# Twelve V buffers in three groups, two more query-weight slices streamed per tile, and a fourth V group in the last two U segments

## The reference, cut to what matters

```python
q = einsum('bsd,de->bse', h, w_query)                 # 1024 -> 2048
scores = einsum('bshpd,hpnd->bshpn', q, sub_keys)     # 8 heads x 2 x 128 keys
...                                                   # top 16 of each, top 16 of their sums
expert = i1 * N_KEYS + i2                             # 8 x 16 = 128 experts for a token
gates = softmax(best)
u = take(expert_u, expert)                            # 128 rows of 1024 floats for a token
act = gelu(einsum('tkd,td->tk', u, x)) * gates
out = einsum('tk,tkd->td', act, take(expert_v, expert))   # another 128 rows of 1024 floats
```

## Time and profile before

| | |
|---|---|
| median of 3 runs | 3504.99 us (3499.11 to 3507.13) |
| the profiled execution | span 3777.3 us; no other time of this execution is given |
| busy, of the span | PE 2191.6 us (58%), DVE 2151.9 (57%), POOL 2096.8 (56%), ACT 384.3 (10%) |
| moved by DMA | 1195.92 MB, mean 317 GB/s |

### The profile page before, as it was taken

One profiled execution on the slowest core, in us unless ns is written; L12 is line 12 of the kernel. 1 busy time (PEld: TensorE's weight loads), 2 busy tenths in 40 slices (PEclk: granted clock), 3 DMA queues, 4 the chain that ended last, 5 costly groups with the idle time before them and its releaser, 6 DMA issues. The chain is left out here.

```text
span 3777.3 us, 34501 instructions
## 1 busy us (share of the span) xinstructions
PE 2191.6 (58%) x9905; PEld 1104.5 (29%) x9905; DVE 2151.9 (57%) x6670; ACT 384.3 (10%) x701; POOL 2096.8 (56%) x2079
## 2 busy tenths in 40 slices
PE   6899968747646656635665455556654333333345
PEld 4666655324233233212321232134211000100111
DVE  4333577565667777568656775667666644444300
ACT  2322132111010010001000100010000000000000
POOL 1000056545635566666666657666666766666664
PEclk9999989877767768766766677756776556555676
DMA  8423288877959899989999999999999999999997
GB/s 281 139 66 102 86 276 328 308 266 283 345 184 330 286 336 378 403 325 352 357 403 353 358 335 404 373 341 354 409 344 360 366 362 363 359 373 361 358 363 296
DMA packets 412550, 1195.92 MB, mean 317 GB/s; under 512 B 58993, under 2 KB 135106, under 8 KB 410434
## 3 DMA queue, kind: packets, MB, share of 16 engines
q0 software_dynamic: 294912, 1073.87, 75.6%
q1 hardware_dynamic: 39970, 75.66, 5.6%
q10 hardware_dynamic: 77472, 44.08, 4.1%
HBM read 1172.46 MB, written 21.00 MB: 316 GB/s over the span
## 5 line engine op out<-in xcount | busy, mean ns | idle before, releaser
L998 POOL DMA_INDIRECT U<-in_expert_u,eidx x1024 | 1054.8, 1030 | 575.6 <-issue 287.5
L1380 PE MATMUL bank<-V,ZH 128*32 128x512 f32 x3712 | 726.3, 897 | 915.9 <-DMA V<-in_expert_v,eidxT 727.5
L2159 DVE CUSTOM_DVE_ANT_0 U<-U,h1c 128x512 f32<-128x512 f32 x1368 | 871.8, 690 | 532.6 <-DMA U<-in_expert_u,eidx 393.7
L1006 POOL DMA_INDIRECT V<-in_expert_v,eidxT x832 | 842.7, 1013 | 499.9 <-POOLq L1004 249.2
L1380 PEld LDWEIGHTS bank<-V,ZH 128*32 128x32 f32 x3712 | 142.0, 142 | 1403.9 <-issue 1401.8
L2148 DVE CUSTOM_DVE_ANT_0 U<-U,h1c 128x1024 f32<-128x1024 f32 x256 | 303.2, 1224 | 67.5 <-DMA U<-in_expert_u,eidx 42.7
L310 PE MATMUL bank<-V,U 128*128 128x387 f32 (+2 forms) x928 | 278.4, 459 | 10.6 <-PEq L308 10.5
L1028 POOL COPY eidx<-eidx_n 128x128 uint32<-128x128 uint32 x8 | 3.3, 413 | 413.9 <-POOLq L1027 413.2
L1185 PE MATMUL bank<-wq,arena 128*128 128x512 f32 x400 | 194.1, 634 | 28.7 <-PEq L1308 18.4
L310 PEld LDWEIGHTS bank<-V,U 128*128 128x128 f32 x928 | 178.9, 196 | 100.5 <-issue 21.6
L372 DVE SCALAR_TENSOR_TENSOR U<-bank,U 128x384 f32<-128x384 f32 (+3 forms) x108 | 61.8, 572 | 127.8 <-DVEq L367 117.2
(11 more groups left out here) (308 smaller groups left out, 2834.6 us busy)
## 6 DMA issues: line engine op xcount, KB each, us to landing
arena<-in_w_out SPq DMA_DIRECT2D x56, 512.0 KB
U<-in_w_in ACTq DMA_DIRECT2D x36, 512.0 KB, 3.9
U<-in_expert_u,eidx POOLq DMA_INDIRECT x1024
V<-in_expert_v,eidxT POOLq DMA_INDIRECT x928
raw<-proj_dram SPq DMA_DIRECT2D x8, 1344.0 KB
wq<-in_w_query SPq DMA_DIRECT2D x4, 2048.0 KB, 15.5
proj_dram<-U ACTq DMA_DIRECT2D x35, 192.0 KB, 1.9
arena<-w_dram SPq DMA_DIRECT2D x6, 1024.0 KB
```

The costliest lines, as they stand in the source:

```text
L998: pool.indirect_dma_start(U[:, c % NU, :], None, expert_u[0], rows(ap=eidx[:, e, c:c + 1], axis=0)).then_inc(g_u[c % NU], 16)
L1006: pool.indirect_dma_start(V[:, c % NV, :], None, expert_v[0], rows(ap=eidxT[:, e, token:token + 1], axis=0)).then_inc(g_v[c % NV // 2], 16)
L1380: last = nc.tensor.matmul(acc_ps[NSTEP * j:NSTEP * j + NSTEP, 512 * n:512 * n + 512], Zb[:, at - i:at - i + NSTEP], buf[j][:, 512 * n:512 ...
L2159: ins = nc.vector.tensor_tensor_reduce(out=U[:, c % NU, lo:lo + D // 2], in0=U[:, c % NU, lo:lo + D // 2], in1=rows[:, lo:lo + D // 2], sc ...
```

## The change

Four things change together. (1) V has 12 buffers in three groups: `V` itself (groups 0 and 1) and the place of `wq`'s slices 5 and 6 (group 2). The table `MIXED_RING` gives the group of each of a tile's 32 steps: 0, 1, 2 by turns up to step 28, then 0, 1, 2, so that the steps 27 to 30 are groups 0, 1, 0, 1. (2) Slices 5, 6 and 7 are all kept in `w_dram` (3 MB, `LEAN` = 3), and each of tiles 2 to 7 reads three slices back instead of one: four transfers where there was one, ahead of the fifth `wo` load, and two more after the last `wo` load, behind a new wait for the second `wo` buffer. PE gives that buffer free after k = 5 too, and waits before `route` for all six. (3) In the last two U segments (V of tiles 5 and 6) the steps go round four groups; the fourth is the first 4096 floats of `arena`, whose token DVE gives when the loop of U segments 2 to 5 is over. (4) ACT's last `fill` of a tile waits for its own end before it tells PE, and SP waits for `s_x_free` too before it loads `wq`.

```diff
+MIXED_RING = [i % 3 for i in range(29)] + [0, 1, 2]
+LAST_RING = [i % 4 for i in range(NSTEP)]
+NRING = 4
+LEAN = 3
...
+def ring_of(t, i):
+
+    return LAST_RING[i] if isinstance(t, int) and t >= T - 3 else MIXED_RING[i]
+
...
-        w_dram = nc.dram_tensor("w_dram", (P, 2 * PH * P), fp32).ap()
+        w_dram = nc.dram_tensor("w_dram", (P, LEAN, 2 * PH * P), fp32).ap()
...
-        w_part = view(1024, 2 * PH * P)
+        w_last, w_next = view(1024, 2 * PH * P), [view(4608, 2 * 512), view(7168, 2 * 512)]
+        w_third = [view(3584, 2 * 512), view(6656, 512), view(3072, 512)]
+
+        def w_read(k, group):
+
+            if k == KD - 1:
+                return w_last[:, 512 * group:512 * group + 512]
+            if k == KD - 2:
+                return w_next[group // 2][:, 512 * (group % 2):512 * (group % 2) + 512]
+            if k == KD - 3:
+                return w_third[0][:, 512 * group:512 * group + 512] if group < 2 else w_third[group - 1]
         Lists = namedtuple("Lists", "top itop ftop cand cid best ibest fbest fex den eq first eq_first")
 
...
+        v_rows = [V[:, 0:4, :], V[:, 4:8, :], wq[:, KD - LEAN:KD - 1, :].rearrange("p k (b d) -> p (k b) d", d=D),
+                  view(0, 4, D)]
...
-                            sp.dma_start(w_part, w_dram[:, :]).then_inc(w_in, 16)
+                            sp.dma_start(w_last, w_dram[:, 2, :]).then_inc(w_in, 16)
+                            sp.dma_start(w_next[0], w_dram[:, 1, 0:1024]).then_inc(w_in, 16)
+                            sp.dma_start(w_next[1], w_dram[:, 1, 1024:2048]).then_inc(w_in, 16)
+                            sp.dma_start(w_third[2], w_dram[:, 0, 1536:2048]).then_inc(w_in, 16)
...
+                    sp.wait_ge(b_wo_free1, 1)
+                    sp.sem_inc(b_wo_free1, -1)
+                    if streamed(t):
+                        sp.dma_start(w_third[0], w_dram[:, 0, 0:1024]).then_inc(w_in, 16)
+                        sp.dma_start(w_third[1], w_dram[:, 0, 1024:1536]).then_inc(w_in, 16)
...
-                def v_row(e, c):
+                def v_row(e, c, ring):
+                    r = ring[c // 4]
                     if c % 4 == 0:
-                        pool.wait_ge(g_vfree[c // 4 % 2], 1)
-                        pool.sem_inc(g_vfree[c // 4 % 2], -1)
+                        pool.wait_ge(g_vfree[r], 1)
+                        pool.sem_inc(g_vfree[r], -1)
                     token = c % 4 * NSTEP + c // 4
-                    pool.indirect_dma_start(V[:, c % NV, :], None, expert_v[0],
-                                            rows(ap=eidxT[:, e, token:token + 1], axis=0)).then_inc(g_v[c % NV // 2], 16)
+                    pool.indirect_dma_start(v_rows[r][:, c % 4, :], None, expert_v[0],
+                                            rows(ap=eidxT[:, e, token:token + 1], axis=0)).then_inc(g_v[2 * r + c % 4 // 2], 16)
 
...
+                with pool.Fori(0, T // 2 - 2):
                     for e in range(2):
-                        next_slots(e)
-                        for q in range(P // 4):
-                            for c in range(4 * q, 4 * q + 4):
...
-                        if k < KD - 3:
+                        if k < KD - 2:
...
-                        pe.wait_ge(w_in, 16)
-                        pe.sem_inc(w_in, -16)
+                        pe.wait_ge(w_in, 16 * 6)
+                        pe.sem_inc(w_in, -16 * 6)
                     for k in range(4 * half, 4 * half + 4):
-                        w = w_part if from_dram and k == KD - 1 else wq[:, k, :]
-                        last = nc.tensor.matmul(o, h1T[:, k, :], w[:, 512 * group:512 * group + 512], start=k == 0, stop=k == KD - 1)
+                        w = w_read(k, group) if from_dram and k >= KD - LEAN else wq[:, k, 512 * group:512 * group + 512]
...
+                    r = i % 2 if wide else ring_of(t, i)
+                    buf = [(U[:, 4 * r + j, :] if in_u else v_rows[r][:, j, :]) for j in range(4)]
                     for c in range(4 * i, 4 * i + 4, 1 if in_u else 2):
-                        pe.wait_ge(g_u[c % NU] if in_u else g_v[c % NV // 2], wide_arrived(t, c) if wide else v_arrived(t, c))
+                        pe.wait_ge(g_u[c % NU] if in_u else g_v[2 * r + c % 4 // 2],
+                                   wide_arrived(t, i, c) if wide else v_arrived(t, i))
...
-                    act.dma_start(w_dram[:, :], wq[:, KD - 1, :]).then_inc(w_stored, 16)
+                    act.dma_start(w_dram[:, :, :], wq[:, KD - LEAN:KD, :]).then_inc(w_stored, 16)
...
-                    nc.scalar.copy(z_columns[:, q % 2, :, :, 0], columns[:, q, :, :]).then_inc(g_zb[q % 2], 1)
+                    last = nc.scalar.copy(z_columns[:, q % 2, :, :, 0], columns[:, q, :, :])
+                    if q < NSTEP // 4 - 1:
+                        last.then_inc(g_zb[q % 2], 1)
+                        return
+                    last.then_inc(s_act, 1)
+                    act.wait_ge(s_act, 1)
+                    act.sem_inc(s_act, -1)
...
+                        if n == 31 and resident:
+                            dve.sem_inc(g_vfree[2], 1)
...
+                for r in range(3, NRING):
+                    dve.sem_inc(g_vfree[r], 1)
```

More of the change, by code:

```diff
@@ L244, in build @@
         s_small = sem("s_small")
-        s_x_free = [sem(f"s_x_free{u}") for u in range(XB)]
         s_tr_free = [sem(f"s_tr_free{u}") for u in range(2)]
@@ L259, in build @@
         gt = sb("gt", [P, 6, T * BH], c=a)
+        s_x_free = [sem(f"s_x_free{u}") for u in range(XB)]
         s_const = sem("s_const")
@@ L447, in _ @@
                 for u in range(XB):
+                    sp.wait_ge(s_x_free[u], 1)
+                    sp.sem_inc(s_x_free[u], -1)
                     sp.wait_ge(s_h_out[u], 16)
@@ L871, in build @@
         g_u = [sem(f"g_u{k}") for k in range(NU)]
-        g_v = [sem(f"g_v{k}") for k in range(NV // 2)]
+        g_v = [sem(f"g_v{k}") for k in range(2 * NRING)]
         g_ufree = [sem(f"g_ufree{k}") for k in range(NU // 2)]
-        g_vfree = [sem(f"g_vfree{k}") for k in range(NV // 4)]
+        g_vfree = [sem(f"g_vfree{k}") for k in range(NRING)]
         w_stored = sem("w_stored")
@@ L917, in u_arrived, with v_arrived, wide_arrived @@
             return (t * 16 + 4 + c // NU) * 16 + 16
-        def v_arrived(t, c):
+        first_fills = [4 * (r < 2) + MIXED_RING[NSTEP // 2:].count(r) for r in range(NRING)]
+        tile_fills = [MIXED_RING.count(r) for r in range(NRING)]
+        def v_arrived(t, i):
+            r = ring_of(t, i)
             if isinstance(t, int) and t == 0:
-                return 32 * (4 + (c - 64) // NV) + 32
-            return (t * 16 - 4 + c // NV) * 32 + 32
-        def wide_arrived(t, c):
-            if c % 16 < 8:
-                return 32 * (108 * (t > 0) + c // 16) + 32
+                return 32 * (4 * (r < 2) + MIXED_RING[NSTEP // 2:i + 1].count(r))
+            if isinstance(t, int) and t >= T - 3:
+                return 32 * (first_fills[r] + (T - 4) * tile_fills[r] + (t - (T - 3)) * LAST_RING.count(r)
+                             + LAST_RING[:i + 1].count(r))
+            return (t * tile_fills[r] + (first_fills[r] - tile_fills[r] + MIXED_RING[:i + 1].count(r))) * 32
+        def wide_arrived(t, i, c):
+            if i % 4 < 2:
+                r = i % 4
+                return 32 * ((first_fills[r] + (T - 4) * tile_fills[r] + 2 * LAST_RING.count(r)) * (t > 0) + i // 4 + 1)
             return 16 * ((132 if t > 0 else 16) + c // 16) + 16
@@ L1036, in next_tokens, with mixed @@
                     pool.sem_inc(g_indexfree, 1)
+                def mixed(e, ring):
+                    next_slots(e)
+                    for q in range(P // 4):
+                        for c in range(4 * q, 4 * q + 4):
+                            u_row(e, c)
+                        for c in range(4 * q, 4 * q + 4):
+                            v_row(1 - e, c, ring)
+                        if q == 3:
+                            next_tokens(e)
                 next_slots(0)
@@ L1051, in _ @@
                     u_row(1, 2 * q + 1)
-                    v_row(0, P // 2 + q)
-                with pool.Fori(0, T // 2 - 1):
+                    v_row(0, P // 2 + q, MIXED_RING)
+                with pool.Fori(0, T // 2 - 2):
                     for e in range(2):
-                        next_slots(e)
-                        for q in range(P // 4):
-                            for c in range(4 * q, 4 * q + 4):
-                                u_row(e, c)
-                            for c in range(4 * q, 4 * q + 4):
-                                v_row(1 - e, c)
-                            if q == 3:
-                                next_tokens(e)
+                        mixed(e, MIXED_RING)
+                for e in range(2):
+                    mixed(e, LAST_RING)
                 for c in range(P):
@@ L1373, in weighted @@
                     in_u = wide and i % 4 >= 2
```

(14 more changed lines are left out.)

2 lines of the change are left out of this document (added).

## The result

The changed kernel takes 3533.84 us (median of 4 runs, 3531.50 to 3534.04), the kernel before 3504.72 us beside it (4 runs, 3499.11 to 3507.13). The ratio is 1.0085, with a 95% interval of 1.0071 to 1.0098: 29 us slower, where 3475 us was forecast.

The account below looks back on a forecast made before the run. It took the DMA engines as the bound, POOL's issuing just under them. Profiled span 3777.3 - 53.4 (V waits) + 21 (streaming) = 3745, times 0.928 = 3475 us, 30 less; 8-in-10 range 3402 to 3525.

Parts of the forecast that it names:

- the 177 us of DMA work that U segments 2 to 7 lack: Idle DMA time in the profile of before, counted as full DMA work; holes that a deeper V could fill.
- B: Rival, more is won: the second kind is V tokens really late, 131 us for both kinds; 3403 us, chance 0.22.
- A: Likeliest case: first-kind V waits go, streaming costs 21 us; 3475 us, own range 3457 to 3500, chance 0.42.
- The first kind of V waits: U segments 2 to 7: POOL resumes about 1 us after the freeing matmuls; 13 waits, all to go, -53.4 us.
- The second kind: 66 waits of 1.2 to 4.5 us before V groups, 202 us, token apparently given earlier; taken as 0, likeliest from profiling.
- The fourth group: U segments 6 and 7: one first-kind wait there, already in the 53.4 us; otherwise 0.
- Streaming for tiles 4 to 7: U segments 2 to 5, engines nearly full: 2.10 MB more a tile, 5.2 us each, +21 us.
- Tiles 2 and 3 hidden in U segment 1, and the save in U segment 0: U segment 1's slack of 78 us hides 10.4 us of streaming; save 0, 5.2 us if not hidden.
- Late weights: Three more transfers ahead of the fifth `wo` load, two before `route`: cover of 17.6 and 50 us, so 0.
- D: Rival, no difference: stream makes `wo` late, piece 18 slips 2 to 13 us a tile, +28 us; 3501 us, chance 0.15.
- C: Rival, slower: DMA engines full in unprofiled runs, each streamed byte adds time; +19 us in the median, 3524 us, chance 0.21.
- The signs: For: first-kind V waits gone, L997 less than doubled, share up 0.02. Against: U segments 6, 7 gaining over 10 us each.

Follow-up runs that it names:

- again: The kernel before, unchanged, run once more with a profile on the first chip: 3799.66 us; median of 18 other runs there 3797.40 us.
- last_only: Kernel before plus a third V group in `arena` in U segments 6 and 7 only, nothing more streamed, second chip: 3501.58 us, ratio 0.9992.
- save_only: Kernel before, but three slices saved once instead of one, nothing more read, third chip: ratio 1.0021 (1.0012 to 1.0030).
- buffers_only: Changed kernel saving and streaming only slice 7 (other routing): against the kernel before 1.0263 on the first chip, 0.9991 on the second (`buffers_only_b`, 3501.15 us).
- stream_none: Kernel before without streaming slice 7, route using slice 6 instead (other experts), third chip: ratio 0.9969 (0.9957 to 0.9981).
- stream_double: Changed kernel with two V groups, plus another 2.10 MB read for each of tiles 2 to 7, first chip: ratio 1.0072 to the kernel before.

## Why the prediction was wrong, step by step

**The step that failed first** is in what bounds the kernel: the 177 us of DMA work that U segments 2 to 7 lack, carried over to the timed runs by the factor 0.928. The 177 us are real in that profile, and `again` has such holes without a profiler's help (3799.66 us against 3797.40 for the others). But they belong to that chip. On the second chip, which times the kernel before as the chip of the result does, `last_only` has a share of 1.01 over U segments 2 to 5 with eight V buffers. Scaling by 0.928 kept the holes in proportion, though they could be up to 177 of the 272 us that separate the profile from the median. The sign was there. The prediction wrote it down ("it can't have all the holes and the same transfers"), used it against B alone, and not against A.

**The first kind of V waits, -53.4 us taken whole.** This is the term that failed. The waits went, as forecast, and on the second chip came back as U waits, 47.8 us for 51.3, the lower bound of 0 that the prediction had named. What it gave as its reason, that "the DVE waits for data (406.9 us) and not the reverse", speaks for the opposite here: consumers that wait for data give tokens at the rate of the data, and a deeper ring only makes POOL wait elsewhere. The 16.41 us of PE behind the chain of pieces have no counterpart: over its whole execution the changed kernel waits 7.7 us in 8 times ahead of that same piece, the longest 1.0.

```profile
PE bank L1165 <- PEq L1307: 7.7, 8, 1.0
```

`last_only` waits 7.0 us in 8 there, so the third group isn't the reason; the chip is the difference that is left.

**The second kind, 0.** Right in size for a wrong reason. That these waits are the profiler's work was argued, and `again` speaks against it: it has them, and takes no longer than runs without a profile. U segment 7 of `again` (3215 to 3586 us) has 40.0 us of V waits in 11:

```profile
POOL V L1006 <- POOLq L1004: 40.0, 11, 4.7
```

On the second and third chip the five kernels with two V groups have none over 0.3 us there, so there was nothing to win. B, 3403 us, is refuted for these chips. The prediction's counts are off here too: 53.4 and 202 us for the two kinds add up to 255.4, where the earlier trace rows has 244.4 for all; 191 would fit. The sum used only the first.

**The fourth group, 0.** Right: `last_only`, which adds buffers in just these segments, gives 0.9992 (0.9983 to 1.0002), and U segment 6 takes 337 us against 338. The reason is one that the prediction had found and not used. It put 333 us for POOL's 256 gathers, and U segment 7 takes 330 in both kernels, with 1.9 us of waits for U tokens. POOL issues without a stop, so in these two segments it bounds the time as well as the bytes do, and no run separates the two.

**Streaming for tiles 4 to 7, +21 us.** Right, 20 us by two ways (1457 against 1437 in the segments, and 0.0057 of 3503 by the ratios).

**Tiles 2 and 3 hidden in U segment 1, and the save in U segment 0, both 0.** Both wrong. U segment 1 grew by 7 us (5 by the ratios), the save costs 7 us (4 to 11 by its interval); forecast were 10.4 and 5.2 for "if not hidden", which was the case. A share of 0.82 was read as slack in which bytes are free. The runs show that they are not; why was not tried. The page's slices in this part swing between 213 and 388 GB/s, so the mean share doesn't tell whether there was room where the bytes lay.

**Late weights, 0.** Right. PE's waits for `wo` are 16.0 us over the whole execution, none over 4.4, and not longer than the 20.2 of `save_only`. D, which had piece 18 late by 2 to 13 us a tile, is refuted with them.

**C is what happened.** Its mechanism was full engines, the waits moving to U, and each byte adding its time; it put 3524 us because it kept the two "hidden" parts at 0. With 5 to 7 for tiles 2 and 3 and 7 for the save, 3505 + 20 + 5 + 7 = 3537, measured 3534. It decides "if more than 60% of the 53.4 us come back as U waits": on the second chip all of them did. Its 3524 lay at the edge of the range, and its chance was 0.21. The Trainium skill, "DMA: Bandwidth & Descriptors", section "Anatomy of one DMA", gives about 2.0 us plus the bytes at 436 GB/s for one transfer issued by GpSimd. From this the prediction worked out, as an estimate, that three gathers in flight fill the engines and more buffers bring nothing. The second chip agrees about the buffers: 1436 us with two groups and with three. It doesn't agree about the figures: the full engines moved 396 to 405 GB/s, and a U gather took 11.3 us from issue to landing, not 3.2. The estimate doesn't cover what the first chip did. That "three V groups lie behind each other", as the prediction says beside it, stands in no row.

**The signs.** Most of the signs that the prediction named for its own case came true, and the kernel is slower all the same. V waits gone, L997's total less than doubled (86.1 to 115.3), share up, `route` as before: all this compares two chips. On one chip the U waits more than doubled, 34.2 to 85.5 us without the stream and 33.6 to 109.2 with it. One sign against it did show: U segments 6 and 7 "gain" 34 and 44 us from one profile to the other, where over 10 was to mean that the prediction is wrong.

**Open.** `buffers_only` is 2.6% slower than the kernel before on the first chip and even with it on the second, with the same program. On the first, POOL waits for U tokens and the engines have holes (share 0.90), but it isn't data that DVE lacks. Over U segments 2 to 5 it waits 31.4 us for U rows, and 42.0 at the same line without a releaser that the profile shows; in `again` these are 149.1 and 36.8. What grew are waits of DVE and PE for each other inside the pieces. One of them is DVE's wait for a product of PE, over U segments 2 to 5 on the first and then on the second chip:

```profile
DVE arena L1842 <- DVEq L1841: 57.0, 7, 14.7
```

```profile
DVE arena L1842 <- DVEq L1841: 5.4, 8, 2.2
```

So there pieces are late; that the U tokens are late behind them is likely, but not followed wait by wait. What makes them late is not shown. Whether depth itself or the changed choice of experts does it there was not separated, and what else ran on the chips is not on record. The changed kernel itself was not run on the first chip, so what the change does where the holes exist is not known; A may hold there or not.

No version beat both kernels by more than the measurement tells: `last_only` and `buffers_only_b` are at 0.9992 and 0.9991. The direction that the runs point to is fewer bytes: `stream_none` shows what not streaming slice 7 would be worth, 0.3% (0.9957 to 0.9981), if a place for it were found.

## What to carry to other kernels

Before idle time of the DMA engines is taken for gain, check that the profile's span agrees with the timed runs: where it differs by some per cent, the holes may be the difference, and must not be scaled along. When, as here, consumers wait for data longer than the issuer waits for tokens, and the share is at its full value, a deeper ring moves the issuer's wait to the next token, and every byte spent on making room for it is paid: here 2.0 to 2.4 us per MB, 29 us in all, for buffers whose own ratio is 0.9991, or 3 us that the runs don't tell from nothing. A mean share of 0.82 to 0.85 was no cover for bytes here; price them, and treat "hidden" as a case with a chance.

## What was not expected of the hardware

One kernel, three Trainium2 chips: 3503, 3503 and 3797 us, each chip's runs of it within 0.8% of their median, at mean granted clocks of TensorE of about 0.76 on the first two and 0.735 on the last. The profile of before has 0.735, that of the changed kernel 0.760. The packets of the same 1073.87 MB of gathers took 3.7% longer on the slow one (2864 against 2762 us), and the rest of the 8% stood as idle time of the DMA engines. Beside it POOL's waits over U segments 2 to 5 were longer: 208.4 us for V tokens and 67.7 for U in `again`, 68.1 and 34.2 in `last_only`. And only the slow chip's profiles have idle time of PE and DVE in these segments that ends with nothing they show, over 100 us of each in `again`; on the others it is 0.2 us at most. Whether that is part of the slowness or only missing from the record is not known. The same edit had other ratios there: the longer stream 1.0023 for 1.0091, the buffers 1.0263 for 0.9991. A profiled execution took the time of an unprofiled one on every chip: none took over 2 us more than the slowest other run of its kernel, and one, `stream_double`, took 24 us less than the fastest.
